# One product behind the sums of squares, made in two halves of 128 columns in three feed-forward stages

## The chip, the cores and the metric

The kernel runs on one core of one Trainium2 chip, in one launch. The metric is the device time of the whole kernel in microseconds (us). Before the change its median over three runs is 2541.31 us (2539.46 to 2542.06).

The engines are named as in the profile: PE is TensorE's matrix multiply, PEld its weight load, DVE is VectorE, ACT is ScalarE, SP issues most of the DMAs. PE and PEld belong to one engine and overlap.

## What is computed

A batch of one sequence of 256 tokens with 1024 channels passes through two models in a row. The first has one layer: a mixer, a cross attention and a mixture of experts (32 experts, 4 per token). The second has four layers. Each of them has an attention and a feed-forward part, and only the feed-forward part is touched here:

```python
def rms_norm(x, g):
    xf = x.astype(jnp.float32)
    y = xf * lax.rsqrt(jnp.mean(xf * xf, axis=-1, keepdims=True) + EPS_2) * g.astype(jnp.float32)
    return y.astype(x.dtype)

def swiglu(h, w_gu, w_out):              # FFN_DIM = 2816
    gu = h @ w_gu
    return (jax.nn.silu(gu[..., :FFN_DIM]) * gu[..., FFN_DIM:]) @ w_out

for i in range(4):                       # second_block
    ...                                  # attention i, added to x
    x = x + swiglu(rms_norm(x, ffn_norm[i]), f_w_gu[i], f_w_out[i])
```

## The kernel before

Activations stand transposed: 128 channels on the partitions, 256 tokens along the free dimension, 8 such blocks for 1024 channels. A weight matrix arrives in units of 128 x 2048 numbers. ACT rounds each unit to a short float (`w_hi`, line 278), DVE takes the rest (`w_lo`, line 285), and the activations are split in the same way into `ht` and `hl`. Each product of the model is then three products on PE: high weights with high activations, low weights with high activations, and high weights with low activations. All of them have 128 x 128 weights and 256 moving columns, and each loads its weights anew.

A feed-forward stage (`ffn_stage`, one for each layer `l` = 0 to 3, called first to fourth here) has 22 blocks of 128 hidden channels. For a block `q`, one weight unit gives the gate half (h = 0) and the value half (h = 1). Each half is a sum over 8 channel blocks `k` with three products each, lines 2063 to 2065 in `next_unit`. Block 0 is made by `project_first` (lines 452, 453, 462). Every two blocks, `out_unit` multiplies the hidden blocks with the output weights (lines 309 to 311 by way of `products`). PE does 16 products of three in each unit, and a stage has 1536 products of 256 columns in all, plus block 0's 48. The middle of the stage is a hardware loop.

The norm's factor is applied after the product. So PE can start on the unnormed activations while the squares are added up: `Hand.square` (ACT), `Hand.reduce` (DVE, gives `ssq`) and `Hand.total` (PE, lines 530 and 532). The total multiplies `ssq` with a matrix of ones for the sum over channels (256 columns, plain f32), and then takes the same sums as columns in two products of 2 columns. ACT takes the root and DVE the reciprocal (`root`, `rstd`), and from then on DVE can evacuate block 0 and block 1.

Where the total stands in PE's order is fixed by the code. PE runs its instructions in program order. In the first, third and fourth stage the total stands in block 1 between the gate half and the value half. In the second stage (`l == 1`) it stands four channel blocks later, in the middle of the value half. Block 2 (`q == 2`) writes into the accumulator of block 0, so its value half waits until DVE has read that (`s_fu`, set by the instruction of line 2138).

Of the kernel before, what the change touches and what calls it, by code (L numbers as in the profile page):

```python
# [14 lines left out]
S = 256  # L15
# [134 lines left out]
def program(nc, x, mem, consts, dft, params, pre, post, router, bgu, bdown, wgu, wdn, out):  # L150
    ctx = ExitStack()
    with ctx:
# [17 lines left out]
        ht, hl = both[:, 0, :, :], both[:, 1, :, :]  # L170
# [128 lines left out]
        def wait_unit(pe, ph, u, i=0, per=0, part=1):  # L299

            pe.wait_ge(ph.lo, 2 * u + part + 1 + 2 * i * per)
# [1689 lines left out]
        def ffn_stage(l, hand, gain, eps):  # L1991
# [45 lines left out]
            def pair_of(q):  # L2037
                return bank_pair[(t0 % 4 // 2 + q) % 2]

            def place(h):  # L2040

                return (t0 + 1 + h) % 2

            def next_unit(pe, u, q, i):

                wait_unit(pe, POST_PH, u, i, UP, part=0)
                if q < 3:
                    pe.wait_ge(s_evac, t0)
                else:
                    pe.wait_ge(s_fu, g0 + q - 1 + i * TP)  # L2050
                wh, wl = (w_[:, u % SR, :].rearrange("p (k n) -> p k n", k=KB) for w_ in (w_hi, w_lo))
                for h in range(2):
                    if h and q == 1 and l != 1:
                        hand.total(pe)
                    if h and q == 2:
                        pe.wait_ge(s_fu, g0 + 1)
                    o, cs = pair_of(q)[:, place(h), 0:S], slice(h * P, (h + 1) * P)
                    for k in range(KB):
                        if k == KB // 2 and h == 0:
                            wait_unit(pe, POST_PH, u, i, UP)  # L2060
                        if k == KB // 2 and h and q == 1 and l == 1:
                            hand.total(pe)
                        pe.matmul(o, wh[:, k, cs], ht[:, k, :], start=(k == 0), stop=False, skip_group_check=True)  # L2063
                        pe.matmul(o, wl[:, k, cs], ht[:, k, :], start=False, stop=False, skip_group_check=True)  # L2064
                        mm = pe.matmul(o, wh[:, k, cs], hl[:, k, :], start=False, stop=(k == KB - 1), skip_group_check=True)  # L2065
                mm.then_inc(post_done, 1)

            def step_pe(pe, j, i=0):
                for u, q, o in in_order(j):
                    if o is not None:  # L2070
                        out_unit(pe, o, i)
                    elif q == 0:
                        project_first(pe, POST_PH, u, t0, "T", hts, hand)
                    else:
                        next_unit(pe, u, q, i)
# [1294 lines left out]
```

## Time and profile before

| what | value |
|---|---|
| median of the three runs | 2541.31 us (2539.46 to 2542.06) |
| the profiled execution | 2533.17 us |
| its span, first to last instruction | 2531.4 us |
| PE busy | 2494.3 us, 99% of the span, 20132 instructions |
| PEld busy | 2064.0 us, 82% |
| DVE busy | 1433.7 us, 57% |
| ACT busy | 1032.2 us, 41% |
| DMA in the feed-forward stages | 160 to 194 GB/s, 47 to 57% of the engines |

The profile is one execution, 8.1 us (0.3%) shorter than the median of the timed ones. The busy time of PE counts overlapping matmuls once, so a busy PE only says that some matmul was always under way. How fast PE goes must be read from the number of matmuls in a stretch. The duration of a matmul's record (0.28 us for 256 columns) is its latency, not its share of the time: the next one starts after about 0.11 us. In the trace a plain f32 product stands as two records, each with its weight load; a product of the split operands stands as one.

### The profile page before, as it was taken

The page shows a single profiled execution, that of the slowest core. Times are in us where ns is not written, and L with a number is a line of the kernel's source. Part 1 is how long each engine was busy: PE and PEld are TensorE (multiplying, and loading weights), DVE is VectorE, ACT ScalarE, POOL GpSimd, SP SyncE. Part 2 cuts the span into 40 slices and gives each one's busy share as a digit, 9 for nine tenths or more (in the row PEclk, how much of TensorE's full clock was granted, in tenths as well). Part 3 has the DMA queues.
Part 4 walks back from the last instruction along what each step waited for, and adds up shares of the span by engine and source line. Part 5 has one row for each costly group of instructions (what it writes and reads, how often), then busy time and mean ns, then how long its engine had stood idle before and what let it go on. Part 6 is the DMA issues. An engine that isn't in the chain of part 4 may idle for free.

```text
span 2531.4 us, 50954 instructions
## 1 busy us (share of the span) xinstructions
PE 2494.3 (99%) x20132; PEld 2064.0 (82%) x20132; DVE 1433.7 (57%) x2911; ACT 1032.2 (41%) x1819; POOL 0.2 (0%) x4
## 2 busy tenths in 40 slices
PE   8999999999999999999999999999999999999998
PEld 7997555556555565558999988999999999999998
DVE  6753333323233323338876687767776776688665
ACT  5443111112121112216754466445455554467444
POOL 0000000000000000000000000000000000000000
PEclk9999999999999999999999999999999999999999
DMA  6456999999999999996355542555654455544552
GB/s 271 167 206 269 419 430 429 429 429 430 429 430 429 429 429 429 429 429 224 127 184 191 179 150 96 192 196 188 209 176 169 144 181 186 185 171 159 183 184 99
DMA packets 71328, 676.13 MB, mean 267 GB/s; under 512 B 8480, under 2 KB 8736, under 8 KB 15648
## 3 DMA queue, kind: packets, MB, share of 16 engines
q1 hardware_dynamic: 64800, 663.84, 67.5%
q10 hardware_dynamic: 6400, 10.49, 1.1%
q8 instruction: 92, 1.51, 0.2%
q14 instruction: 36, 0.29, 0.0%
HBM read 662.76 MB, written 1.05 MB: 262 GB/s over the span
## 4 chain that ended last, share of the span: by engine, by line
PE 91%; ACT 4%; DVE 3%; issue 1%; ACTq 1%; DMA 0%; DVEq 0%; SPq 0%
PE bank L2873 18%; PE bank_pair L2891 9%; PE bank_pair L2065 6%; PE bank_pair L2063 6%; PE bank_pair L2064 6%; PE bank_pair L309 6%; PE bank_pair L311 6%; PE bank_pair L310 6%; PE bank_pair L2863 5%; PE bank L309 4%; PE bank L311 4%; PE bank L310 4%; PE bank_pair L2880 2%; PE bank L2937 1%; PE bank_pair L2937 1%
## 5 line engine op out<-in xcount | busy, mean ns | idle before, releaser
L278 ACT ACTIVATE w_hi<-ring 128x1024 fp32r<-128x1024 f32 (+1 forms) x486 | 495.2, 1049 | 481.3 <-PE bank_pair L2065 213.8
L285 DVE TENSOR_TENSOR w_lo<-ring,w_hi 128x1024 fp32r<-128x1024 f32 (+1 forms) x488 | 581.6, 1217 | 173.7 <-ACT w_hi L278 173.2
L2063 PE MATMUL bank_pair<-ht,w_hi 128*128 128x256 f32 x1344 | 376.6, 280 | 0.0
L2064 PE MATMUL bank_pair<-ht,w_lo 128*128 128x256 f32 x1344 | 376.1, 280 | 0.0
L2065 PE MATMUL bank_pair<-ht,w_hi 128*128 128x256 f32 x1344 | 376.1, 280 | 0.0
L2064 PEld LDWEIGHTS bank_pair<-ht,w_lo 128*128 128x128 f32 x1344 | 256.6, 191 | 0.0
L2065 PEld LDWEIGHTS bank_pair<-ht,w_hi 128*128 128x128 f32 x1344 | 252.4, 188 | 0.0
L2063 PEld LDWEIGHTS bank_pair<-ht,w_hi 128*128 128x128 f32 x1344 | 252.3, 188 | 0.1
L3078 DVE TENSOR_SCALAR big<-bank_pair,big 128x64 f32<-128x64 f32 x256 | 60.8, 279 | 330.1 <-PE bank_pair L2880 330.1
L2873 PE MATMUL bank<-ring,big 128*64 128x256 f32 x2048 | 235.1, 382 | 0.1
L2873 PE MATMUL bank<-moe_w,big 128*64 128x256 f32 x2048 | 235.2, 382 | 0.0
L309 PE MATMUL bank_pair<-ht,w_hi 128*128 128x256 f32 x768 | 219.4, 286 | 1.9 <-DVE w_lo L285 1.9
L311 PE MATMUL bank_pair<-ht,w_lo 128*128 128x256 f32 x768 | 214.2, 279 | 0.0
L310 PE MATMUL bank_pair<-ht,w_hi 128*128 128x256 f32 x768 | 214.2, 279 | 0.0
L2965 ACT ACTIVATE big<-bank 128x256 f32<-128x256 f32 x128 | 49.2, 384 | 397.5 <-PE bank L2873 397.5
L2873 PEld LDWEIGHTS bank<-ring,big 128*64 128x64 f32 x2048 | 141.3, 137 | 80.6 <-issue 15.6
L2873 PEld LDWEIGHTS bank<-moe_w,big 128*64 128x64 f32 x2048 | 141.7, 137 | 75.1 <-issue 10.8
L309 PE MATMUL bank<-hid_hi,w_hi 128*128 128x256 f32 x704 | 196.9, 280 | 0.0
L310 PE MATMUL bank<-hid_lo,w_hi 128*128 128x256 f32 x704 | 196.9, 280 | 0.0
L311 PE MATMUL bank<-hid_hi,w_lo 128*128 128x256 f32 x704 | 196.9, 280 | 0.0
L3110 DVE TENSOR_TENSOR xt<-xt,bank 128x512 f32<-128x512 f32 x66 | 42.4, 684 | 269.3 <-PE bank L2937 269.3
L309 PEld LDWEIGHTS bank_pair<-ht,w_hi 128*128 128x128 f32 x768 | 144.6, 188 | 6.6 <-DVE w_lo L285 3.0
(418 smaller groups left out, 4698.5 us busy)
## 6 DMA issues: line engine op xcount, KB each, us to landing
ring<-post SPq DMA_DIRECT2D x213, 1024.0 KB, 4.9
ring<-wgu SPq DMA_DIRECT2D x64, 2048.0 KB, 13.9
moe_w<-wgu SPq DMA_DIRECT2D x64, 2048.0 KB, 15.6
big<-wdn SPq DMA_DIRECT2D x32, 2048.0 KB, 17.8
moe_w<-wdn SPq DMA_DIRECT2D x32, 2048.0 KB, 16.5
ring<-pre SPq DMA_DIRECT2D x27, 1024.0 KB, 5.0
prob<-probt ACTq DMA_DIRECT2D x64, 128.0 KB, 3.5
ring<-post SPq DMA_DIRECT2D x3, 768.0 KB, 4.3
```

What stands on the lines that cost most here:

```text
L278: act.activation(w_hi[:, u % SR, cs], ring[:, u % R, cs], ACT.Copy).then_inc(ph.hi, 1)
L285: dve.tensor_tensor(w_lo[:, u % SR, cs], ring[:, u % R, cs], f32(w_hi[:, u % SR, cs]), ALU.subtract).then_inc(ph.lo, 1)
L309: pe.matmul(out, wh, xh, start=start and k == k0, stop=False, **kw)
L310: pe.matmul(out, wh, xl, start=False, stop=False, **kw)
L311: mm = pe.matmul(out, wl, xh, start=False, stop=stop and k == k1 - 1, **kw)
L2063: pe.matmul(o, wh[:, k, cs], ht[:, k, :], start=(k == 0), stop=False, skip_group_check=True)
L2064: pe.matmul(o, wl[:, k, cs], ht[:, k, :], start=False, stop=False, skip_group_check=True)
L2065: mm = pe.matmul(o, wh[:, k, cs], hl[:, k, :], start=False, stop=(k == KB - 1), skip_group_check=True)
L2863: mm = pe.matmul(bank[6][:, d * CAP:(d + 1) * CAP], h2[:, t_, d * P:(d + 1) * P], sel[:, t_, :], start=(t_ == 0), stop=(t_ == 1))
L2873: mm = pe.matmul(bank[2 + f % 2][CAP * half:CAP * half + CAP, 0:S], xg[:, k, :], w[:, k, half, :], start=(k == 0), stop=(k == KB - 1))
L2891: mm = pe.matmul(bank[7][CAP * half:CAP * half + CAP, :], hid[:, 2 * m + k2, :], w[:, 2 * (m % 2) + k2, half, :], start=(m == 0 and k2 == ...
L3078: ins = dve.tensor_scalar(g_s[:, f % 2, c_ * CAP:(c_ + 1) * CAP], bank[4 + f % 2][:, c_ * P:c_ * P + CAP], own_bias[:, 2 * f + c_:2 * f + ...
```

## The change

In `next_unit`, for block 1, value half, channel block `k == 1`, the first of the three products (high weights, high activations) is made as two: columns 0 to 127 and columns 128 to 255, with the same weights and into the same accumulator. It is done in the first, third and fourth feed-forward stage (`l != 1`). It is the fourth product behind the total. All sums stay the same.

```diff
                         if k == KB // 2 and h and q == 1 and l == 1:
                             hand.total(pe)
-                        pe.matmul(o, wh[:, k, cs], ht[:, k, :], start=(k == 0), stop=False, skip_group_check=True)
+                        for c0, c1 in ((0, 128), (128, S)) if k == 1 and h and q == 1 and l != 1 else ((0, S),):
+                            pe.matmul(o[:, c0:c1], wh[:, k, cs], ht[:, k, c0:c1], start=(k == 0), stop=False, skip_group_check=True)
                         pe.matmul(o, wl[:, k, cs], ht[:, k, :], start=False, stop=False, skip_group_check=True)
```

On PE, around the total of the first feed-forward stage, the order before was this (the new code has one line more, so its line numbers are one higher):

```order
L2065 MATMUL bank_pair<-ht,w_hi 128x256
L530 MATMUL bank<-ssq,con 128x256
L532 MATMUL bank<-con,ssq 128x2 x2
L2063 MATMUL bank_pair<-ht,w_hi 128x256
L2064 MATMUL bank_pair<-ht,w_lo 128x256
L2065 MATMUL bank_pair<-ht,w_hi 128x256
L2063 MATMUL bank_pair<-ht,w_hi 128x256
L2064 MATMUL bank_pair<-ht,w_lo 128x256
L2065 MATMUL bank_pair<-ht,w_hi 128x256
```

And with the change it is this:

```order
L2066 MATMUL bank_pair<-ht,w_hi 128x256
L530 MATMUL bank<-ssq,con 128x256
L532 MATMUL bank<-con,ssq 128x2 x2
L2064 MATMUL bank_pair<-ht,w_hi 128x256
L2065 MATMUL bank_pair<-ht,w_lo 128x256
L2066 MATMUL bank_pair<-ht,w_hi 128x256
L2064 MATMUL bank_pair<-ht,w_hi 128x128 x2
L2065 MATMUL bank_pair<-ht,w_lo 128x256
L2066 MATMUL bank_pair<-ht,w_hi 128x256
```

One row of 256 columns has become one of 128 columns that stands twice. The same happens in the third and the fourth stage. Nothing else moves, on this engine or another, and no wait is added or taken away.

## Rows read from the trace of the kernel before

**Rows 1.** Page, parts 1 and 2: busy time of PE, granted clock in 40 slices.

```profile
PE 2494.3 (99%) x20132; PEld 2064.0 (82%) x20132; DVE 1433.7 (57%) x2911; ACT 1032.2 (41%) x1819; POOL 0.2 (0%) x4
...
PEclk9999999999999999999999999999999999999999
```

**Rows 2.** Page, part 4: the chain that ended last, share of the span by engine.

```profile
PE 91%; ACT 4%; DVE 3%; issue 1%; ACTq 1%; DMA 0%; DVEq 0%; SPq 0%
```

**Rows 3.** Windows: first, third, fourth, second feed-forward stage; busy us (xinstructions), clock, DMA share, GB/s.

```profile
1281.40:1459.60 178.20, 178.20 (x1515) 178.20 (x1514) 117.47 (x177) 80.99 (x111) 0.00 (x0) 1.00 0.54 183
2035.40:2213.50 178.10, 178.10 (x1514) 178.04 (x1512) 117.41 (x176) 80.89 (x111) 0.00 (x0) 1.00 0.54 183
2341.80:2519.50 177.70, 177.70 (x1511) 177.70 (x1510) 115.72 (x174) 81.91 (x115) 0.00 (x0) 1.00 0.47 160
1585.20:1747.80 162.60, 162.60 (x1437) 162.60 (x1437) 110.10 (x166) 76.25 (x104) 0.00 (x0) 1.00 0.56 194
```

**Rows 4.** Timeline of PE, first stage, around the total: start us, us, instruction.

```profile
1280.23 0.59 PE L530 MATMUL bank<-ssq,con 128*128 128x256 f32 x2
1280.66 0.50 PE L532 MATMUL bank<-con,ssq 128*128 128x2 f32 x4
1281.02 0.36 PE L2063 MATMUL bank_pair<-ht,w_hi 128*128 128x256 f32 x1
1281.22 0.28 PE L2064 MATMUL bank_pair<-ht,w_lo 128*128 128x256 f32 x1
...
1281.46 0.28 PE L2063 MATMUL bank_pair<-ht,w_hi 128*128 128x256 f32 x1
```

**Rows 5.** Timeline of PE, behind the totals of the third and the fourth stage.

```profile
2034.85 0.36 PE L2063 MATMUL bank_pair<-ht,w_hi 128*128 128x256 f32 x1
2035.05 0.28 PE L2064 MATMUL bank_pair<-ht,w_lo 128*128 128x256 f32 x1
...
2341.23 0.36 PE L2063 MATMUL bank_pair<-ht,w_hi 128*128 128x256 f32 x1
2341.43 0.28 PE L2064 MATMUL bank_pair<-ht,w_lo 128*128 128x256 f32 x1
```

**Rows 6.** Timeline of PE and PEld, second stage, where its pace changes.

```profile
1584.16 0.28 PE L2065 MATMUL bank_pair<-ht,w_hi 128*128 128x256 f32 x1
1584.23 0.19 PEld L2063 LDWEIGHTS bank_pair<-ht,w_hi 128*128 128x128 f32 x1
1584.28 0.34 PE L2063 MATMUL bank_pair<-ht,w_hi 128*128 128x256 f32 x1
...
1584.45 0.28 PE L2064 MATMUL bank_pair<-ht,w_lo 128*128 128x256 f32 x1
...
1584.92 0.28 PE L2065 MATMUL bank_pair<-ht,w_hi 128*128 128x256 f32 x1
...
1585.03 0.28 PE L2063 MATMUL bank_pair<-ht,w_hi 128*128 128x256 f32 x1
```

**Rows 7.** Timeline of PE: short products in a row, in the mixture of experts.

```profile
220.73 1.50 PE L2863 MATMUL bank_pair<-big 128*128 128x64 f32 x12
```

**Rows 8.** Timeline of PE: two other interruptions, ahead of the fourth and behind the first stage.

```profile
2320.64 0.30 PE L309 MATMUL bank_pair<-a_out_hi,w_hi 128*128 128x256 f32 x1
2320.77 0.28 PE L310 MATMUL bank_pair<-a_out_lo,w_hi 128*128 128x256 f32 x1
2320.89 0.28 PE L311 MATMUL bank_pair<-a_out_hi,w_lo 128*128 128x256 f32 x1
2321.01 0.28 PE L309 MATMUL bank_pair<-a_out_hi,w_hi 128*128 128x256 f32 x1
...
1460.46 0.50 PE L462 MATMUL bank_pair<-ht,w_hi 128*128 128x256 f32 x2 [0.64 <-DVE ht L512]
...
1461.03 0.28 PE L452 MATMUL bank_pair<-ht,w_hi 128*128 128x256 f32 x1
1461.14 0.28 PE L453 MATMUL bank_pair<-ht,w_lo 128*128 128x256 f32 x1
```

## The prediction

> **What bounds the kernel now.** I read the page first: PE is busy 99% of the span at a granted clock of nine tenths or more in every slice [rows 1], and the chain that ended last runs over PE for 91% [rows 2]. So what counts is how fast PE goes through its matmuls, and where something makes it stop. In the four feed-forward stages it does not stop: in the windows of all four it is busy from end to end, at clock 1.00 [rows 3]. DVE (65 to 68%) and ACT (45 to 47%) have room there, and the DMA engines are half idle.
>
> The reader should next divide time by instructions, because busy time hides the pace. A window counts every matmul that overlaps it, so its first ones began up to 0.28 us earlier, and that much is added to its length. The first stage gives 178.48 us / 1515 = 117.8 ns from one matmul to the next. The third gives 178.38 / 1514 = 117.8 ns, the fourth 177.98 / 1511 = 117.8 ns. The second gives 162.88 / 1437 = 113.35 ns [rows 3]. It is the same code with the same shapes, the same clock and more DMA traffic (194 GB/s against 160 to 183), and yet each matmul is 4.45 ns (3.8%) shorter. PE has two paces here, and each holds for about 1500 matmuls and through a hardware loop. The slow one is not a limit of the work.
>
> Where does a pace begin? In the first stage the total ends with short products, the next long one is recorded with 0.36 us in place of 0.28, and from then on the starts are 0.12 us apart (1281.22 to 1281.46 is two of them) [rows 4]. The third and the fourth stage show the same rows to 0.01 us [rows 5]. In the second stage the total stands elsewhere, and soon behind it a weight load begins late: 0.07 us after the matmul ahead (1584.23 against 1584.16), where otherwise the two begin together. The matmul that it serves is recorded with 0.34 us, the next starts 0.17 us later, and some four matmuls on the starts are 0.11 apart [rows 6] and stay so for the 1437 of the window. So a small irregularity of some 0.05 us in the stream of loads and matmuls moved PE from the slow pace to the fast one.
>
> **The change part by part.** It removes three matmuls of 256 columns and adds six of 128. Nothing waits newly, and no DMA, ACT or DVE instruction moves. Two terms follow.
>
> The first is the direct cost. Each half has its own weight load of 128 columns. Short products in a row show what a load costs when there is little to stream: twelve of 64 columns take 1.50 us, so (1.50 - 0.28) / 11 = 0.111 us each [rows 7]. A half of 128 columns streams in less than this, so it costs a load: about 0.11 us for the additional pair, less 0.007 for each neighbour that is then bound by its load and not by the slow pace. That is +0.10 us a stage, +0.3 us in all. Nothing else of the before trace shows a 128-column product of these split operands, so I bound it. If the second half found its weights in place and were free, it would be 0, and there is no reason for less, since the same columns are streamed. From above, if narrow products of this kind were treated as plain f32, each half would cost up to a whole plain f32 record of 256 columns: the two of line 530 take 0.59 us, so the second starts 0.59 - 0.38 = 0.21 us after the first [rows 4], where 0.38 is the length of one. Two halves would be 0.42 less 0.12 = +0.31 us a stage, +0.9 us in all. I take +0.3, which comes from the nearest row in shape.
>
> The Trainium skill ("TensorE: Matmul & The Clock Gate", section "Back-to-back issue gap") gives the isolated gap of a warm matmul as N / 2.4 + 2.5 ns, so 109 ns for 256 columns and 56 for 128. By that, two halves would cost 112 against 109, practically nothing, and there would be one pace for each width. The trace disagrees on both: short products keep 111 ns [rows 7], and 256 columns have two paces at one clock [rows 3].
>
> The second term is the pace. In the new stream the first half streams only half as long, so the matmul of the second half is accepted about 0.05 us before its weights are in, and the load for the product after it starts about 0.05 us after that matmul is recorded as begun. The following long matmul should again be recorded about 0.05 us too long, with 0.17 us to the next. That is nearly the picture of the second stage's late load (0.34 us, then 0.17) [rows 6], and unlike the picture behind the total (0.36, then 0.20) [rows 4], after which the slow pace sets in. So I expect the split to do on purpose what the late load did by chance. What it is worth: behind the split the three stages have 1515 + 1514 + 1511 = 4540 matmuls in the windows [rows 3], less about five each until the pace settles, 4525 x 4.45 ns = 20.1 us. All of it would be seen in the time, because PE is never idle in those windows. What is late next is known as well: the second stage runs at the fast pace with DVE 68% busy and DMA at 56%, and PE still waits for nothing.
>
> The sum: -20.1 + 0.3 = -19.8 us. The profiled execution would go from 2533.2 to 2513.4 us. The median lies 8.1 us above it. I can't say from the trace where these 8.1 us are, so I carry them over: 2541.3 - 19.8 = 2521.5 us.
>
> **The rivals.**
> *The pace stays slow in all three.* For it: behind the totals the slow pace sets in again and again, and the split stands only three products behind one, its shorter chain of loads being of the same kind. A short interruption also works the other way: ahead of the fourth stage a start comes late (2320.77 after 2320.64, 0.13), and the starts behind it are 0.12 apart [rows 8]. Against: behind the first stage a wait is followed by 0.11 us (1461.03, 1461.14) [rows 8], so an interruption ends the slow pace as often as not. Time: 2541.3 + 0.3 = 2541.6 us. The skill's single gap for each width, above, would lead here as well.
>
> *Only one or two stages change.* Their rows behind the total are alike to 0.01 us [rows 4, 5], which speaks for one answer in all three. But the fill of the queue and what DVE and ACT do at that moment differ. Each stage is worth about 6.7 - 0.1 = 6.6 us: 2534.9 with one, 2528.3 with two.
>
> *The second stage loses its pace, and the others gain none: slower.* Its fast pace hangs on one late load of some 0.05 us that comes from DVE's read of an accumulator. If what stands before shifts PE against DVE there by more than this, the late load is gone and the slow pace of its total goes on. Place: 1584.2 us; price: 1437 x 4.45 ns and about 70 more in the rest of the stage, 6.7 us. It decides the sign only if none of the three other stages turns fast: 2541.3 + 0.3 + 6.7 = 2548.3 us. Against: the stages between pass through waits of their own that absorb a shift of 0.1 us. The upper bound of the split (+0.9 us) alone stays at 2542.2, which is no change.
>
> **How the numbers follow.** All three stages turn fast: 0.48. One or two do: 0.13. None does: 0.29. Slower by the second stage, or an attention stage that falls into the slow pace: 0.10. The time is that of the first case, 2521.5 us. Its own range is 2517 to 2526, for the settling, the cost of the split and the 8.1 us that I carried. The range for 8 in 10 must reach the case without effect, and on the low side it must allow that an attention stage picks up a little too: 2517 to 2543. A measurement of this kernel can tell about 0.2% (5.1 us) from no change. One stage alone (6.6 us) is just above it. So faster gets 0.48 + 0.12 = 0.60, the same 0.31, slower 0.09.
>
> **What would show it.** In the profile after, the windows of the first, third and fourth stage should hold about 1572 matmuls in 178 us, and the stages should end some 6.6 us sooner each. The starts behind the halves should be about 0.17 and then 0.12 or 0.11 apart. The two halves should stand as two records of line 2064 with 128x128; four records would mean the plain f32 treatment and the upper bound. If the starts return to 0.118 us within ten matmuls, the pace was not touched, and the time is that of the first rival. The forecast is wrong in its root if the pace turns fast and the stages are no shorter, which would mean that DVE, ACT or the weights' arrival takes the time back.

## The result and the profile after

The changed kernel takes 2519.1 us (median of three runs, 2512.5 to 2520.2) against 2541.31 us before. The ratio is 0.9907, with a 95% interval of 0.9879 to 0.9934, so it is faster by 22 us (0.9%). The profiled execution took 2512.5 us in place of 2533.17, its span 2510.6 in place of 2531.4. The forecast was 2521.5 us for the median and 2513.4 for the profiled execution.

The page of the changed kernel shows little of this. Part 1 and part 4:

```profile
PE 2472.3 (98%) x20135; PEld 2042.5 (81%) x20135; DVE 1434.3 (57%) x2911; ACT 1031.8 (41%) x1819; POOL 0.2 (0%) x4
...
PE 91%; ACT 4%; DVE 3%; issue 1%; ACTq 1%; DMA 0%; DVEq 0%; SPq 0%
```

PE is busy for 22 us less with three records more, and the chain's shares are those of [rows 2]. The other engines did the same work. The windows of the changed kernel say where the time went: the first, third, fourth and second feed-forward stage, with the columns of [rows 3] (us, then busy us and instructions of PE, PEld, DVE, ACT, POOL, the granted clock, the DMA share, GB/s).

```profile
1283.00:1453.00 170.00, 170.00 (x1501) 169.88 (x1499) 115.91 (x176) 80.77 (x110) 0.00 (x0) 1.00 0.55 191
2029.00:2199.00 170.00, 170.00 (x1502) 170.00 (x1502) 115.94 (x175) 80.63 (x109) 0.00 (x0) 1.00 0.56 192
2329.00:2499.00 170.00, 170.00 (x1501) 169.97 (x1500) 114.66 (x175) 82.04 (x114) 0.00 (x0) 1.00 0.49 167
1573.00:1743.00 170.00, 169.15 (x1490) 168.78 (x1490) 117.41 (x180) 81.29 (x113) 0.00 (x0) 1.00 0.57 194
```

Divide as before: (170 + 0.28) / 1501 = 113.4 ns from one matmul to the next in the first stage, 113.4 in the third and in the fourth, where [rows 3] gave 117.8. The clock is 1.00 as before. The last row can't be divided like the others: its window reaches 2.5 us past the last product of the second stage and takes in a wait of PE behind it. From its total to its last output product the second stage takes 171.22 us, and it took 171.21 before, so it was fast and is fast here.

The timeline of PE in the first stage, from the total on, shows where the pace turns. It answers to [rows 4].

```profile
1280.08 0.59 PE L530 MATMUL bank<-ssq,con 128*128 128x256 f32 x2
1280.51 0.50 PE L532 MATMUL bank<-con,ssq 128*128 128x2 f32 x4
1280.88 0.36 PE L2064 MATMUL bank_pair<-ht,w_hi 128*128 128x256 f32 x1
1281.08 0.28 PE L2065 MATMUL bank_pair<-ht,w_lo 128*128 128x256 f32 x1
1281.19 0.28 PE L2066 MATMUL bank_pair<-ht,w_hi 128*128 128x256 f32 x1
1281.31 0.34 PE L2064 MATMUL bank_pair<-ht,w_hi 128*128 128x128 f32 x2
1281.48 0.33 PE L2065 MATMUL bank_pair<-ht,w_lo 128*128 128x256 f32 x1
1281.66 0.28 PE L2066 MATMUL bank_pair<-ht,w_hi 128*128 128x256 f32 x1
...
1282.24 0.28 PE L2065 MATMUL bank_pair<-ht,w_lo 128*128 128x256 f32 x1
1282.35 0.28 PE L2066 MATMUL bank_pair<-ht,w_hi 128*128 128x256 f32 x1
1282.47 0.28 PE L2064 MATMUL bank_pair<-ht,w_hi 128*128 128x256 f32 x1
1282.58 0.28 PE L2065 MATMUL bank_pair<-ht,w_lo 128*128 128x256 f32 x1
```

Up to 1281.31 it is the picture of before. The two halves stand as two records. The full product behind them is recorded with 0.33 us in place of 0.28, and the next starts 172 ns later (1281.66 after 1281.48 in rounded times). From 1282.24 on three steps take 0.34 us, so 0.113 each. Those are the lengths that the late load of the second stage showed before (0.34, then 0.17) [rows 6].

From the start of the total to the start of the last output product, the three stages took 178.84 us each before and take 172.27 each now. So each gained 6.57 us, 19.7 us in all. The remaining 1.1 us of the 20.8 in the span lie outside them.

### The profile page after: what moved, and what is told of

Same layout as the page of the kernel before. It is cut to its first block, busy times and chain, and to the rows that moved or that the text cites. A ratio compares the mean times of both kernels' runs of the same rounds, so it can differ in the third digit from the quotient of the medians.

```text
span 2510.6 us, 50960 instructions
## 1 busy us (share of the span) xinstructions
PE 2472.3 (98%) x20135; PEld 2042.5 (81%) x20135; DVE 1434.3 (57%) x2911; ACT 1031.8 (41%) x1819; POOL 0.2 (0%) x4
## 4 chain that ended last, share of the span: by engine, by line
PE 91%; ACT 4%; DVE 3%; issue 1%; ACTq 1%; DMA 0%; DVEq 0%; SPq 0%
PE bank L2874 18%; PE bank_pair L2892 9%; PE bank_pair L2064 6%; PE bank_pair L2065 6%; PE bank_pair L2066 6%; PE bank_pair L309 6%; PE bank_pair L310 6%; PE bank_pair L311 6%; PE bank_pair L2864 5%; PE bank L309 4%; PE bank L311 4%; PE bank L310 4%; PE bank_pair L2881 2%; PE bank L2938 1%; ACT w_hi L278 1%
## 5 line engine op out<-in xcount | busy, mean ns | idle before, releaser
L2064 PE MATMUL bank_pair<-ht,w_hi 128*128 128x256 f32 (+1 forms) x1347 | 372.3, 277 | 0.1
L2066 PE MATMUL bank_pair<-ht,w_hi 128*128 128x256 f32 x1344 | 371.7, 277 | 0.0
L309 PE MATMUL bank_pair<-ht,w_hi 128*128 128x256 f32 x768 | 219.2, 285 | 2.2 <-DVE w_lo L285 2.2
L310 PE MATMUL bank_pair<-ht,w_hi 128*128 128x256 f32 x768 | 214.0, 279 | 0.0
```

The source lines that it names most:

```text
L309: pe.matmul(out, wh, xh, start=start and k == k0, stop=False, **kw)
L310: pe.matmul(out, wh, xl, start=False, stop=False, **kw)
L2064: pe.matmul(o[:, c0:c1], wh[:, k, cs], ht[:, k, c0:c1], start=(k == 0), stop=False, skip_group_check=True)
```

## The experiments

Each kernel is given by its difference from the changed kernel, or from the one before where that is said. Theory A, as in the prediction: the short stream puts an irregularity of some 0.05 us into the run of loads and matmuls, this turns PE from the slow pace to the fast one, and the pace then holds. "Stage length" is the time from the start of the total to the start of the last output product, read from the timeline: 178.8 at the slow pace and 172.3 at the fast one. In the second stage it is 177.4 and 171.2, because its total stands later.

**The split in the first stage alone**

```diff
-if k == 1 and h and q == 1 and l != 1
+if k == 1 and h and q == 1 and l == 0
```

> The split stands in the first feed-forward stage alone. Theory A (each split turns its own stage from the slow pace, 117.8 ns from one matmul to the next, to the fast one, 113.3 ns, by the irregularity it puts into the stream of loads and matmuls; the pace then holds to the end of the stage): the first stage takes 175.1 us from its first line-2064 product to its last output product in place of 181.7, the third and fourth stay at 181.7; the time is 2541.3 - 6.6 = 2534.7 us. Theory C (the gain came from something that the three stages share, or from chance of the run, and not from the split in its place): the three stages move together, all at about 175 or all at 181.7.

Measured: 2533.01 us, ratio to before 0.9981 (0.9971 to 0.9991). Its windows, in the order first, second, third, fourth stage:

```profile
1292.00:1432.00 140.00, 140.00 (x1238) 140.00 (x1236) 93.20 (x139) 64.72 (x87) 0.00 (x0) 1.00 0.56 189
1582.00:1722.00 140.00, 140.00 (x1191) 140.00 (x1190) 90.62 (x136) 62.55 (x84) 0.00 (x0) 1.00 0.55 187
2046.00:2186.00 140.00, 140.00 (x1191) 140.00 (x1190) 89.80 (x136) 61.83 (x84) 0.00 (x0) 1.00 0.53 183
2352.00:2492.00 140.00, 140.00 (x1191) 140.00 (x1191) 89.81 (x134) 61.80 (x83) 0.00 (x0) 1.00 0.53 182
```

In 140 us the first stage makes 1238 matmuls, and the third and fourth make 1191 as before. So the split acts in its own stage, and theory C falls. All ten runs lie within 2532.18 to 2533.74 us. The kernel before, beside them, has a median of 2538.78 and a spread of 2532.04 to 2541.32, so the medians are 5.8 us apart where one stage is worth 6.6. But the second stage, whose code is the same in all of these kernels, is slow here too (length 177.42 in place of 171.21). That was not expected by either theory, and it is followed up below.

**No split, the total moved as in the second stage** (from the kernel before)

```diff
-                    if h and q == 1 and l != 1:
-                        hand.total(pe)
...
-                        if k == KB // 2 and h and q == 1 and l == 1:
+                        if k == KB // 2 and h and q == 1:
                             hand.total(pe)
```

> No product is split; the total of the first, third and fourth stage is moved four channel blocks later, to where the second stage has it. Theory A': the irregularity need not be a split. With the later total DVE's reading of the accumulator is late for block 2's value half, as in the second stage, a weight load begins some 0.05 us late, and from there the fast pace holds: each stage some 6.3 us shorter (the slow pace holds for about 60 matmuls first), 2541.3 - 19 = 2522 us. Rival: only a short stream changes the pace, a late load was a coincidence: 2541 us, 117.8 ns throughout in the three stages.

Measured: 2539.2 us, ratio 1.0006 (0.9995 to 1.0017). All four stages were slow, with a length of 177.42 each. The expectation failed, but not in favour of its rival: the timeline shows no late load in any of the four, so nothing put an irregularity into the stream. DVE freed the accumulator in time. In the second stage it was close (the section on the changed kernel again says how close), and in the three others there were 0.48 us to spare. So this profile doesn't test whether a late load turns the pace. Two of the ten runs, at 2533.36 and 2533.95 us, are as much shorter than the rest as one fast stage would make them, but they were not profiled.

**The split one product later**

```diff
-for c0, c1 in ((0, 128), (128, S)) if k == 1 and h and q == 1 and l != 1 else ((0, S),):
-    pe.matmul(o[:, c0:c1], wh[:, k, cs], ht[:, k, c0:c1], ...)
-pe.matmul(o, wl[:, k, cs], ht[:, k, :], ...)
+pe.matmul(o, wh[:, k, cs], ht[:, k, :], ...)
+for c0, c1 in ((0, 128), (128, S)) if k == 1 and h and q == 1 and l != 1 else ((0, S),):
+    pe.matmul(o[:, c0:c1], wl[:, k, cs], ht[:, k, c0:c1], ...)
```

> The split is moved by one product: the product of the low weights with the high activations of channel block 1 is made as two of 128 columns, in the three stages. Theory A: what counts is the short stream, not which product; same as the change, 175.0 us in each of the three stages and about 2520 us. Rival D: the fast pace is reached only from a certain place (the slow pace repeats itself every three matmuls, 353.3 ns, so a split one product later meets it in another phase): one or more of the stages stay at 181.7 us, up to 2541.6 us.

Measured: 2516.73 us, ratio 0.9925 (0.9901 to 0.9948); lengths 172.26, 172.28 and 172.26. So it need not be the first of the three products. The third was not tried.

**One product made twice at full width**

```diff
-((0, 128), (128, S)) if k == 1
+((0, S), (0, S)) if k == 1
```

> The same product is made twice with its full 256 columns, so that the accumulator of block 1 holds it twice: this part of the output is not the reference's. The same number of instructions as with the split, but no short stream. Theory A: no irregularity, so the slow pace stays: 181.7 + 0.12 us a stage, 2541.3 + 0.35 = 2541.7 us. Rival B: one more pair of load and matmul is enough (a count or a parity in the stream): 175 us a stage and about 2521 us.

Measured: 2539.25 us, ratio 1.0002 (0.9993 to 1.0012); lengths 178.96 in all three stages. The timeline of PE in the first stage:

```profile
1281.54 0.28 PE L2066 MATMUL bank_pair<-ht,w_hi 128*128 128x256 f32 x1
1281.65 0.40 PE L2064 MATMUL bank_pair<-ht,w_hi 128*128 128x256 f32 x2
1281.89 0.28 PE L2065 MATMUL bank_pair<-ht,w_lo 128*128 128x256 f32 x1
1282.01 0.28 PE L2066 MATMUL bank_pair<-ht,w_hi 128*128 128x256 f32 x1
1282.13 0.28 PE L2064 MATMUL bank_pair<-ht,w_hi 128*128 128x256 f32 x1
```

The two start 0.12 us apart, the product behind them is recorded with its usual 0.28 us, and the steps stay at 0.12. The additional pair costs its 0.12 us (178.96 - 178.84), and nothing turns. So it is not the count of instructions, and rival B falls. What the split has besides the additional pair is needed: two short products in place of a long one.

**Two splits in a stage**

```diff
-if k == 1 and h
+if k in (1, 4) and h
```

> In each of the three stages a second product is split as well, the first of channel block 4, nine products behind the first split. The first split alone brings the fast pace within five matmuls. Theory A1 (a split always leaves the fast pace behind it, whatever the pace ahead): 113.3 ns to the end, 172.3 + 0.1 us from total to last output product, about 2517 to 2520 us. Rival A2 (a split changes the pace, so a second one brings the slow one back): 178.9 us, 2541.5 us.

Measured: 2516.91 us, ratio 0.9925 (0.9906 to 0.9944); lengths 172.40 each. The second split met a stream at the fast pace and left it there, at a cost of 0.13 us. It does not toggle.

**The split about 100 matmuls further on, in block 3**

```diff
-if k == 1 and h and q == 1 and l != 1
+if k == 1 and h and q == 3 and i is 0 and l != 1
```

> The split is moved away from the total: to the value half of block 3, about 100 matmuls further on. Theory A (the split acts where it stands, on whatever stream is there): 117.8 ns up to it, 113.3 from it on; each of the three stages 172.3 + 0.45 us from its total to its last output product. Rival E (only the stream just behind the total, where the pace has not settled, can be turned): 178.9 + 0.1 us, no gain, 2541 us.

Measured: 2515.1 us, ratio 0.992 (0.9901 to 0.9939); lengths 172.70 each. The timeline of PE in the first stage:

```profile
1293.13 0.28 PE L2065 MATMUL bank_pair<-ht,w_lo 128*128 128x256 f32 x1
1293.25 0.28 PE L2066 MATMUL bank_pair<-ht,w_hi 128*128 128x256 f32 x1
1293.37 0.34 PE L2064 MATMUL bank_pair<-ht,w_hi 128*128 128x128 f32 x2
1293.54 0.33 PE L2065 MATMUL bank_pair<-ht,w_lo 128*128 128x256 f32 x1
1293.71 0.28 PE L2066 MATMUL bank_pair<-ht,w_hi 128*128 128x256 f32 x1
...
1294.30 0.28 PE L2065 MATMUL bank_pair<-ht,w_lo 128*128 128x256 f32 x1
1294.41 0.28 PE L2066 MATMUL bank_pair<-ht,w_hi 128*128 128x256 f32 x1
1294.52 0.28 PE L2064 MATMUL bank_pair<-ht,w_hi 128*128 128x256 f32 x1
```

Steps of 0.12 stand ahead of the split, steps of 0.11 from 1294.30 on. The pace was settled slow for 100 matmuls and still turned. The price of waiting is 172.70 - 172.27 = 0.43 us, which is 96 x 4.45 ns, and the split stands 96 matmuls later. (`i is 0` in the edit is true outside the hardware loop, where block 3 stands, so it changes nothing.)

**64 and 192 columns in place of 128 and 128**

```diff
-((0, 128), (128, S))
+((0, 64), (64, S))
```

> The product is made as one of 64 and one of 192 columns. The short stream is now one of 64 columns, so the second part is accepted about 0.08 us before its weights are in, but it streams for 0.08 us itself, and the next product is accepted only 0.03 us early. Theory A with no matter of size: fast pace, 172.3 us in each of the three stages. Rival F (the irregularity must be about 0.05 us at the first full product, as with the late load and with the two halves): the slow pace stays, 178.9 us, 2541 us. I give F 0.4.

Measured: 2520.68 us, ratio 0.9943 (0.9924 to 0.9962). The first and the fourth stage turned (172.27), the third did not (178.94). The timeline of PE behind the halves, in the first stage and then in the third:

```profile
1280.77 0.36 PE L2064 MATMUL bank_pair<-ht,w_hi 128*128 128x64 f32 x2
1280.96 0.31 PE L2065 MATMUL bank_pair<-ht,w_lo 128*128 128x256 f32 x1
1281.11 0.28 PE L2066 MATMUL bank_pair<-ht,w_hi 128*128 128x256 f32 x1
...
2028.00 0.36 PE L2064 MATMUL bank_pair<-ht,w_hi 128*128 128x64 f32 x2
2028.20 0.30 PE L2065 MATMUL bank_pair<-ht,w_lo 128*128 128x256 f32 x1
2028.34 0.28 PE L2066 MATMUL bank_pair<-ht,w_hi 128*128 128x256 f32 x1
```

The same code gave a step of 0.15 us in the one and 0.14 in the other (143 and 136 ns in the trace), and only the first turned the pace. Neither theory holds as it was put. Nor is it shown that 136 ns was too small a step: the step ahead of it was longer in return (175 ns against 169), so that the three steps from the first part on take 340 ns in the third stage and 341 in the first. What decided between the two stages stays open.

**A split in the second stage as well**

```diff
-if k == 1 and h and q == 1 and l != 1
+if k == (5 if l == 1 else 1) and h and q == 1
```

> The three splits as in the change, and one in the second feed-forward stage, again in the channel block behind the total (which stands at block 4 there, so the split is in block 5). In the profiled run of the changed kernel a late load brought the second stage its fast pace; in three of four other profiles there was no late load, and it stayed slow for 177.4 us. Theory G (the two groups of times, about 6 us apart, in every kernel so far are the second stage's late load, there or not): with the split all runs fall into one group, at 2512 to 2514 us, and all four stages take 171 to 172.4 us. Rival H (the groups have another cause, such as the weights' arrival in the mixture of experts): two groups again, 2513 and 2520 us.

> The kernel with a split in each of the four stages again, unaltered, beside the changed kernel. If the second stage's late load is what the split replaces, its upper group should hold fewer runs than that of the changed kernel, and its median lie 0 to 5 us lower; if the spread has another cause, the medians are equal within 1 us.

Measured in the first set: 2515.69 us, ratio 0.9922 (0.9907 to 0.9938). In the second: 2520.05 us, ratio 0.994 (0.9925 to 0.9955), beside 2514.28 us for the changed kernel. Both profiled executions showed four fast stages (171.03 to 172.27) and took 2513.65 and 2512.4 us. But six of the ten runs lay between 2518.2 and 2521.4. So theory G did not hold in this form: this split did not remove the upper group. In both profiles the late load stands in the second stage all the same, 57 products behind the split, and there it left the fast pace in place.

**The changed kernel again**

> The changed kernel again, unaltered, for its spread beside the others on the same chip. Theory G: its runs fall into two groups, near 2513 and near 2520 us, and if the profile catches one of the upper group it shows one feed-forward stage at 177.4 or 178.9 us. Rival H: the feed-forward stages are at 171 to 172.4 us in either group, and the time is lost elsewhere, such as in the mixture of experts (917.5 us in every profile so far).

Measured: 2514.28 us, ratio 0.9915 (0.99 to 0.993). Four runs lay between 2512.3 and 2514.9 and one, the profiled one, at 2519.05. Its windows, first, second, third and fourth stage:

```profile
1292.00:1432.00 140.00, 140.00 (x1238) 140.00 (x1237) 93.04 (x140) 64.71 (x88) 0.00 (x0) 1.00 0.56 190
1582.00:1722.00 140.00, 140.00 (x1191) 140.00 (x1190) 90.59 (x136) 62.55 (x84) 0.00 (x0) 1.00 0.55 188
2045.00:2185.00 140.00, 140.00 (x1238) 140.00 (x1237) 93.00 (x140) 64.71 (x88) 0.00 (x0) 1.00 0.56 190
2345.00:2485.00 140.00, 140.00 (x1237) 140.00 (x1237) 92.99 (x140) 64.70 (x88) 0.00 (x0) 1.00 0.55 188
```

Here the second stage is the slow one: 177.42 us in place of 171.22, which is 6.2 of the 6.6 us between this execution and the profiled one of the result. The mixture of experts took 917.46 us in both, so rival H falls for this kernel. No late load stands in the second stage here, nor in the other three profiles with a slow second stage. One stands there in each of the six profiles whose second stage was fast without a split in it. They are those of the kernel before, of the changed kernel's first profile, of the split one product later, of two splits in a stage, of the split in block 3, and of 64 columns. In four of them it is where the pace turns. In the changed kernel's first profile and in that with two splits, the fast pace stood already ten records behind the total, with no split there, and the late load left it in place.

How a late load comes about can be read from DVE's rows. It is the first load of block 2's value half, which waits until DVE has read block 0's accumulator (line 2138 before the change). In all ten profiles with a late load, it begins 115 to 117 ns after that instruction of DVE ended. In the four without one it begins 125 to 137 ns after it. So PE misses the wait there by 10 to 20 ns, and small differences between executions decide. PE also comes to this place earlier when the stream ahead of it is fast: in all six profiles in which it was fast there (two without a split in the second stage, four with one) the load was late, against four of the eight in which it was slow.

**Splits at nine more places**, in the mixer, the cross attention, the latent attention, the product of the memory's keys and the output products, besides all four stages

```diff
-def products(pe, out, w, x, k0, k1, start, stop, rest=None, **kw):
+def products(pe, out, w, x, k0, k1, start, stop, rest=None, cut=None, **kw):
...
-                pe.matmul(out, wh, xh, start=start and k == k0, stop=False, **kw)
+                for c0, c1 in ((0, 128), (128, S)) if k == cut else ((0, out.shape[-1]),):
+                    pe.matmul(out[:, c0:c1], wh, xh[:, c0:c1], start=start and k == k0, stop=False, **kw)
```

> Splits in all four feed-forward stages and at nine more places where the profile of the changed kernel shows a long slow stretch (behind the totals of the mixer, the cross attention and the latent attention, in the product of the memory's keys and in the output products of the attentions). Theory A: each of them turns its stretch: together some 900 matmuls by 4.45 ns = 4.0 us, less 9 x 0.1 = 0.9 us for the splits, so 3 us below the kernel with four splits: about 2511 to 2513 us, and a lowest run near 2510.5. Rival: in these stages PE waits for ACT or DVE soon after, which takes the time back: no gain, or up to 0.9 us slower.

Measured: 2521.32 us, ratio 0.9934 (0.9916 to 0.9953), with the lowest run at 2513.32. So there was no gain. Six of the nine turned their stretch within ten matmuls. Five of these stretches end at the next wait or the next plain f32 product, and the sixth ends without either (below); they last from 7 to some 115 matmuls. The three others did not turn theirs: behind the split in the mixer 20 more steps are slow, behind that in the memory's keys all 91 up to the next plain f32 product, and behind that in the output products ahead of the first stage some 115. In the last two, the steps from the first half on are 60, 109 and 171 ns. In the second feed-forward stage of the same profile they are 60, 109 and 173, and there the pace turned. So the steps that the timeline shows at a split don't tell whether it works. In the feed-forward stages all 32 splits of 128 columns that met the slow pace turned it, over all profiles; outside them six of nine did. The profiled execution (2521.79 us) shows one way in which a kernel with four splits comes into an upper group. In its second stage the split worked (the fast pace stood after twelve records), and 55 matmuls later PE met this. The timeline of PE and PEld:

```profile
1578.23 0.28 PE L2066 MATMUL bank_pair<-ht,w_lo 128*128 128x256 f32 x1
...
1578.35 0.28 PE L2067 MATMUL bank_pair<-ht,w_hi 128*128 128x256 f32 x1
1578.54 0.19 PEld L2065 LDWEIGHTS bank_pair<-ht,w_hi 128*128 128x128 f32 x1
1578.57 0.36 PE L2065 MATMUL bank_pair<-ht,w_hi 128*128 128x256 f32 x1
...
1578.76 0.28 PE L2066 MATMUL bank_pair<-ht,w_lo 128*128 128x256 f32 x1
...
1579.00 0.28 PE L2065 MATMUL bank_pair<-ht,w_hi 128*128 128x256 f32 x1
1579.12 0.28 PE L2066 MATMUL bank_pair<-ht,w_lo 128*128 128x256 f32 x1
1579.23 0.28 PE L2067 MATMUL bank_pair<-ht,w_hi 128*128 128x256 f32 x1
```

The load at 1578.54 is late by 0.19 us: block 2's value half waits for DVE. The steps behind are 0.12, and in the rest of the stage 1440 matmuls went at the slow pace (length 177.58). The load at the same place, late by 0.07 us, turned a slow stage fast before [rows 6]. So an interruption can turn the pace either way, and a split ahead of one is not safe.

The pace also turns where nothing interrupts the stream. The same profile shows it ahead of the fourth stage, in the stretch that a split had turned fast at 2313.78. The output products end, and block 0 of the stage begins (line 453 here):

```profile
2326.93 0.28 PE L311 MATMUL bank_pair<-a_out_lo,w_hi 128*128 128x256 f32 x1
2327.04 0.28 PE L312 MATMUL bank_pair<-a_out_hi,w_lo 128*128 128x256 f32 x1
2327.15 0.28 PE L453 MATMUL bank_pair<-ht,w_hi 128*128 128x256 f32 x1
2327.27 0.28 PE L454 MATMUL bank_pair<-ht,w_lo 128*128 128x256 f32 x1
2327.39 0.28 PE L453 MATMUL bank_pair<-ht,w_hi 128*128 128x256 f32 x1
2327.51 0.28 PE L454 MATMUL bank_pair<-ht,w_lo 128*128 128x256 f32 x1
```

Steps of 0.11 become steps of 0.12, no load is late, and the pace stays slow up to the total. The 14 profiles have 70 such passages from a mixer's or an attention's output products into block 0 of what follows, none with a step over 120 ns or a load more than 5 ns late. In all 21 that were reached at the fast pace it turned slow. Of the 49 reached at the slow pace, 17 turned fast.

**Two splits in each of the four stages**, the second in block 3, behind that wait

```diff
-if k == (5 if l == 1 else 1) and h and q == 1
+if h and (q == 1 and k == (5 if l == 1 else 1) or q == 3 and k == 1)
```

> All four feed-forward stages have a split behind the total and a second one in the value half of block 3, about 100 matmuls on. With one split in each stage the times still fell between 2513.7 and 2520.8 us, though all four stages were fast in the profiled run. Theory I (in some executions one stage is not turned by its split and stays slow for 6.6 us): the second split catches it, and all runs lie at 2514 to 2516 us (0.4 us dearer for the four splits). Rival H (the spread of 6 us has another cause that these stages don't hold): runs at 2514 and at 2520 us as before.

Measured: 2515.1 us, ratio 0.992 (0.9905 to 0.9935), all five runs between 2514.18 and 2516.11. There was no upper group in five runs, where one split in each of the four stages had six in ten. That is as theory I said, and the profile above gives a mechanism that fits. It is no proof that no run falls out, and this kernel's median is not below the changed kernel's in the same set (2514.28). The changed kernel with one more split, at block 3 of the second stage, would have four splits fewer and so be about 0.4 us cheaper by estimate (0.10 to 0.13 us each). It was not run.

## Why the prediction was right, and where not

**The pace (forecast -20.1 us).** Right in what it does and in size. Three stages turned, and 3 x 6.57 = 19.7 us came of it with the splits' cost already in it, against 19.8 forecast. The steps came as described: the product behind the halves is recorded 0.05 us too long, then comes a step of 0.17, and then about five records until the pace settles. One split alone gave one stage alone. An equal count without a short stream gave nothing. The reason given, that an irregularity of some 0.05 us turns the pace, is only in part borne out: a late load of about that size did so in four profiles, but splits with much the same steps left the pace slow at three of nine places outside the feed-forward stages.

**The direct cost (+0.10 us a stage).** Right in size. From the start of the halves (1281.31) to the product behind the next two (1281.77 in the trace) it is 0.46 us, where three full products at the slow pace took 0.353. A further split in a fast stream cost 0.13 us. The upper bound, plain f32 treatment, is excluded by the two records. The isolated gaps of the Trainium skill ("TensorE: Matmul & The Clock Gate", section "Back-to-back issue gap"), by which two halves would cost 112 ns against 109, and which the page gives for single matmuls and not for a stream with weight loads, are not what these runs show: the second half starts 61 ns after the first and the next product 112 ns after that, but the one behind it only after 172.

**The rivals.** "Stays slow in all three" was wrong for 128 columns. That one stage stayed slow with 64 columns, and three stretches outside the feed-forward stages with 128, shows that it was not far off. Nothing in the rows of before told that the feed-forward stages would turn every time. The rival of the second stage named a real mechanism. In the ten profiles without a split there, the stage is fast just where a late load stands, for 6.2 us in place of the 6.7 that I worked out. It does not follow from the change, though: the kernel before has both groups too. Beside the first set of experiments, 25 of its runs spread from 2532.04 to 2541.32 us.

**The 8.1 us that I carried over.** I could not place them, and this was the step that hid something. The profiled execution of before was one with a fast second stage. If the three timed runs had a slow one, as their times suggest, its 6.2 us are most of the 8.1. So a median of three runs, before or after, depends on how many of the three had it, and it was luck that both medians fell in the upper group. In the later set the changed kernel's median was 2514.28 us, which is below the forecast's range of 2517 to 2543, and that of before was 2533.78. Their difference is 19.5 us. The result's medians are 22.2 us apart and the profiled executions 20.7. The figure for the change itself is the 19.7 us in its three stages.

**What stands between the stages.** I set it to nothing, and it was -1.1 us. Counting steps of 116 to 123 ns, the stretch between the second and the third stage has 753 slow ones where before it had 1083, and the one ahead of the fourth 483 in place of 624. The attention stages change pace at many of their waits and passages, and where they do differs between executions: the changed kernel's second profile has 861 and 563 there.

**What stays open.** Why PE has two paces at one clock, and what in it remembers which, was not settled. The runs show some of what turns it, not what it is, and not why the same split or the same passage turns it at one time and not at another. That the upper group of the kernels with four splits is always the late load of the second stage rests on one profile.

## What to carry to other kernels

Divide a busy window by its count of matmuls before calling an engine full: here two paces 4% apart hid under "99% busy, clock 1.00" and were worth 20 us. If an equal stage runs at another pace elsewhere in the program, look at where the pace begins; a product with a short stream, made at no cost in accuracy, can set it. Look in the profile whether it did, and how far it holds: a late load, a plain f32 product or the passage to another group of products can turn the pace back. And where runs fall into groups, find by the profile which stage differs before a median is compared with another or a single profile's time is carried over.

## What the runs showed of the hardware

- A stream of 128 x 128 loads and 256-column products on the split operands has two steady paces at granted clock 1.00: 117.8 and 113.4 ns. Each held for about 1500 matmuls, through a hardware loop and semaphore waits that did not stop PE.
- A product of 256 columns made as two of 128 turned the slow pace fast in 32 of 32 cases in the feed-forward stages; it left a fast one fast. At nine places outside them it did so six times (profile with more splits). As 64 and 192 columns it turned two stages of three.
- Of the interruptions of DVE's making, loads late by 39, 41, 63 and 69 ns (steps of 145 to 173 ns) turned slow to fast. Loads late by 106, 106, 157, 303 and 307 ns left the fast pace in place, and one late by 193 ns turned it slow. So the size alone does not decide it.
- The plain f32 products of a total left the slow pace behind them in all 57 cases in which none of the nine steps ahead was over 126 ns, three of them behind a fast stream. Where a longer step stood there (a wait or a plain f32 product), they left the fast pace in 38 of 62 cases. Totals with a split close behind are not counted.
- The pace turned with no late load and no step over 120 ns at 38 of 70 passages from output products into the next block 0.
